# Gathered experts' down products as three fp32r passes, adaLN two pieces per step in the full experts, two more split gate blocks, and moved steps

## What is computed

```python
# first block, after the residual: 4 groups of 8 experts, top-1 group, top-2 experts in it
for n in range(N_EXPERTS):                       # 32 experts, 1024 -> 2 x 256 -> 1024
    a, b = jnp.split(h @ w_up[n], 2, axis=-1)
    out = out + combine[:, n:n + 1] * ((jax.nn.silu(a) * b) @ w_down[n])
# second block, per layer
mod = (silu(c) @ w_ada[l] + b_ada[l]).reshape(B, N_MOD, D_MODEL)       # adaLN
hn = rms_norm(h, g_ffn1[l]) * (1.0 + sc1) + sh1
h = h + 0.5 * (1.0 + gt1) * swiglu(hn, w_ffn1_in[l], w_ffn1_out[l])
```

## Time and profile before

| what | value |
|---|---|
| median of 3 runs | 1892.06 us |
| the profiled execution | 1889.99 us |
| its span, first to last instruction | 1888.2 us |
| TensorE busy | 1841.8 us (98%) |
| VectorE busy | 1173.6 us (62%) |
| ScalarE busy | 780.9 us (41%) |
| mean granted TensorE clock | 0.994 of full |
| read from and written to memory | 206 GB/s over the span |

### The profile page before, as it was taken

The page is one execution under the profiler, slowest core; times in us unless marked ns, Lnnn a source line. Parts: engine busy times, 40 slices in busy tenths (PEclk is TensorE's granted clock), DMA queues, the critical chain, the costliest instruction groups (busy, mean ns, idle before and its releaser), DMA issues.

```text
span 1888.2 us, 29939 instructions
## 1 busy us (share of the span) xinstructions
PE 1841.8 (98%) x12476; PEld 1661.0 (88%) x12476; DVE 1173.6 (62%) x1777; ACT 780.9 (41%) x1081; POOL 0.2 (0%) x4
## 2 busy tenths in 40 slices
PE   9999999899999999999999999999999999989999
PEld 8879889788866668999988889999999997879999
DVE  3875456566666656877547458776876547545543
ACT  2325442534444445434443234344443444324432
POOL 0000000000000000000000000000000000000000
PEclk9999999899999999999999999999999999999999
DMA  8334311566899986876530057876686341043451
GB/s 316 132 130 158 137 68 35 239 233 241 321 395 370 376 320 236 342 302 260 199 134 23 23 204 287 331 301 258 256 320 253 157 157 45 6 152 133 181 201 68
DMA packets 65222, 391.59 MB, mean 207 GB/s; under 512 B 7360, under 2 KB 7488, under 8 KB 27328
## 3 DMA queue, kind: packets, MB, share of 16 engines
q1 hardware_dynamic: 64800, 389.61, 53.4%
q10 hardware_dynamic: 288, 0.08, 0.0%
HBM read 388.61 MB, written 1.05 MB: 206 GB/s over the span
## 4 chain that ended last, share of the span: by engine, by line
PE 88%; DVE 7%; ACT 2%; issue 1%; DMA 1%; DVEq 0%; SPq 0%; ACTq 0%
PE bank L510 87%; DVE region L2219 1%; PE bank L551 1%; ACT w_hi L1452 1%; DMA slab<-in_w_ffn_in 1%; DVE slab_low L1900 0%; DVE region L2182 0%; DMA slab<-in_w_up 0%; DVE region L1913 0%; DVE tiny L2181 0%; DVE region L2505 0%; DVE region L2482 0%; DVE region L2503 0%; DVE region L2173 0%; DVE region L2501 0%
## 5 line engine op out<-in xcount | busy, mean ns | idle before, releaser
L1900 DVE TENSOR_TENSOR slab_low<-slab,w_hi 128x2048 fp32r<-128x2048 f32 x152 | 348.2, 2292 | 201.8 <-ACT w_hi L1452 201.5
L510 PE MATMUL bank<-h_hi,w_hi 128*128 128x256 f32 x1408 | 391.6, 281 | 0.0
L510 PE MATMUL bank<-h_hi,slab_low 128*128 128x256 f32 x1408 | 390.9, 281 | 0.0
L510 PE MATMUL bank<-h_lo,w_hi 128*128 128x256 f32 x1408 | 380.2, 281 | 0.0
L1452 ACT ACTIVATE w_hi<-slab 128x2048 fp32r<-128x2048 f32 x152 | 291.0, 1916 | 151.1 <-DMA slab<-in_w_ffn_in 72.9
L510 PEld LDWEIGHTS bank<-h_hi,slab_low 128*128 128x128 f32 x1408 | 269.5, 191 | 0.0
L510 PEld LDWEIGHTS bank<-h_hi,w_hi 128*128 128x128 f32 x1408 | 264.7, 188 | 0.4
L510 PEld LDWEIGHTS bank<-h_lo,w_hi 128*128 128x128 f32 x1408 | 257.6, 188 | 0.0
L510 PE MATMUL bank<-gT_hi,d_hi 128*128 128x256 f32 x832 | 234.0, 281 | 0.8 <-DVE gT_lo L2097 0.8
L510 PE MATMUL bank<-gT_lo,d_hi 128*128 128x256 f32 x832 | 233.7, 281 | 0.0
L510 PE MATMUL bank<-gT_hi,d_low 128*128 128x256 f32 x832 | 233.6, 281 | 0.0
(11 more groups left out here) (279 smaller groups left out, 2826.0 us busy)
## 6 DMA issues: line engine op xcount, KB each, us to landing
slab<-in_w_ffn_in SPq DMA_DIRECT2D x88, 1024.0 KB, 8.6
slab<-in_w_up SPq DMA_DIRECT2D x64, 1024.0 KB, 8.8
region<-in_w_ada SPq DMA_DIRECT2D x112, 512.0 KB, 6.6
region<-in_w_ffn_out SPq DMA_DIRECT2D x44, 1024.0 KB, 4.8
region<-in_w_down SPq DMA_DIRECT2D x32, 1024.0 KB, 5.5
slab<-in_w_in SPq DMA_DIRECT2D x23, 1024.0 KB, 4.8
slab<-in_w_mix_in SPq DMA_DIRECT2D x20, 1024.0 KB, 7.9
hT<-in_w_ada SPq DMA_DIRECT2D x32, 512.0 KB, 5.7
```

What stands on the lines that cost most here:

```text
L510: return nc.tensor.matmul(o, lhsT, rhs, start=start, stop=True, skip_group_check=True)
L1900: V_.tensor_tensor(slab_low[slot][:, :], slab[slot][:, :], w_hi[h % 3][:, :].bitcast(F), ALU.subtract)\
```

## The change

- `down_few` becomes three fp32r passes: ScalarE converts each gathered expert's down weights (`down_high` at the end of its own step), VectorE subtracts them (`down_low`, right behind `hidden`) and makes `gT_lo` for these experts too; `d_hi` alternates between two buffers, `gT_few` goes, and `permT` moves to `rsB` and the router's weights. `bank_free` waits for `gt_lo` for every expert.
- `ada_slot` gives two pieces per step in the experts' stage: 32 pieces in steps 1 to 16. `ADA_PLAN`'s rate, the two places and the order of SyncE's loads stay.
- `GATES_PLAIN` goes from 4 to 2: 22 gate blocks of 24 are split, in 11 slabs.
- In stage 1 the rotations of q and k (`qka_normed`) come after all 16 blocks, and the doubled keys after the four key blocks; VectorE makes `in_lo` and the first gate slab's low part ahead of the norms of the memory's q and k.
- At the start of the experts: `keep_warm(5)` becomes 3; ScalarE brings in `htok_lo` and `permT` ahead of `up_high(0)`; c is loaded after the second unit's up weights.

```diff
@@ -162,7 +162,7 @@
...
 GATHER_PLACES = 3
-GATES_PLAIN = 4
+GATES_PLAIN = 2
 VALUES = P + 8
...
@@ -181,10 +181,6 @@
...
     halves: list
-
-    @property
-    def split(self):
-        return self.kind != "few"
...
@@ -223,7 +219,7 @@
...
     _, _, n, rate = ADA_PLAN[seg]
-    return [p for p in range(n) if 1 + p // rate == r]
+    return [p for p in range(n) if 1 + p // (rate if seg else 2) == r]
...
@@ -367,7 +363,7 @@
...
         second = zone(27 * KB + NT * N_EXP, NT * PER_GROUP).rearrange("p (t e) -> p t e", t=NT)
-        permT = zone(28 * KB, (N_GROUP - 1) * T).rearrange("p (i t) -> p i t", i=N_GROUP - 1)
+        permT = [rsB[:, 0:T], rsB[:, T:2 * T], part["router"][:, 0:T]]
         hg_hi, hg_lo = split_zone("hg_hi", 72 * KB, [KD, GS]), split_zone("hg_lo", 84 * KB, [KD, GS])
...
@@ -378,8 +374,6 @@
...
         gT_lo = [parts_at(f"gT_lo{b}", [2, T], silu_at + 4096 * b + 2048) for b in range(2)]
-        gT_few = [nc.alloc_sbuf_tensor_at(f"gT_few{b}", [P, 2, P], F, offset=silu_at + 4096 * b)
-                  for b in range(2)]
         act_s, gu_s = lnt[:, 0:T], lnt[:, T:2 * T]
...
@@ -463,11 +457,7 @@
...
-            return sum(len([x for x in u.steps if x <= s]) for u in UNITS if u.split)
-
-        def split_units(u):
-
-            return sum(1 for x in UNITS[:u + 1] if x.split)
+            return s + 1
...
@@ -486,7 +476,7 @@
...
-            return 0 if unit.seg == 0 else unit.u % 2
+            return 0 if unit.kind == "full" else (unit.u + 1) % 2
...
@@ -759,10 +749,8 @@
...
                     pe.wait_ge(S["gut"], old + 1)
-                elif unit.split:
+                else:
                     pe.wait_ge(S["gt_lo"], low_steps(old))
-                else:
-                    pe.wait_ge(S["gt_hi"], old + 1)
...
@@ -794,7 +782,7 @@
...
                 b = unit.u % 2
-                pe.wait_ge(S["dlo_ready"], split_units(unit.u))
+                pe.wait_ge(S["dlo_ready"], unit.u + 1)
                 pe.wait_ge(S["gt_lo"], low_steps(unit.steps[-1]))
...
@@ -813,15 +801,18 @@
...
                 b = unit.u % 2
-                pe.wait_ge(S[f"d_in{b}"], 16 * (unit.u // 2 + 1))
-                pe.wait_ge(S["gt_hi"], unit.steps[-1] + 1)
+                pe.wait_ge(S["dlo_ready"], unit.u + 1)
+                pe.wait_ge(S["gt_lo"], low_steps(unit.steps[-1]))
                 if unit.x == 0 and unit.group > 1:
                     pe.wait_ge(S["y_copied"], 2 * (unit.group - 1))
-                rows_ = d_raw[b].rearrange("p (j d) -> p j d", j=2)
+                hi = d_hi[d_hi_of(unit)][:, :].rearrange("p (j d) -> p j d", j=2)
+                lo = d_low[b][:, :].rearrange("p (j d) -> p j d", j=2)
                 for j in range(2):
                     for half in range(2):
-                        m = mm(bank[2 + half][:, :], gT_few[b][:, j, :], rows_[:, j, half * 512:(half + 1) * 512],
-                               unit.x == 0 and j == 0)
+                        o, cols = bank[2 + half][:, :], slice(half * 512, (half + 1) * 512)
+                        mm(o, gT_hi[b][:, j, 0:P], hi[:, j, cols], unit.x == 0 and j == 0)
+                        mm(o, gT_hi[b][:, j, 0:P], lo[:, j, cols])
+                        m = mm(o, gT_lo[b][:, j, 0:P], hi[:, j, cols])
                     if j == 0 and middle:
...
@@ -833,13 +824,13 @@
...
                     m = mm(bank[4 + d // 2][:, (d % 2) * T:(d % 2 + 1) * T], y_few[:, d * P:(d + 1) * P],
-                           permT[:, i - 1, :])
+                           permT[i - 1])
                     if i == N_GROUP - 1:
...
             def down(unit, middle=None):
-                if unit.split:
+                if unit.kind != "few":
                     down_split(unit, unit.steps[0] == SLOTS_OF[unit.seg][0][2], middle,
...
@@ -848,7 +839,7 @@
...
                 slabs_of(members[0])
-                keep_warm(5)
+                keep_warm(3)
                 for s in range(2):
...
@@ -983,21 +974,17 @@
...
                     pair_sum(sq[:, 5, :])
-                if b == 15:
-                    pe.wait_ge(S["qka_normed"], w("qka_normed"))
-                    for x in range(2):
-                        pair_sum(B1["qa"][:, 2 * x:2 * x + 2, :], "rot", "dve")
-                    pair_sum(B1["ka"], "rot", "dve")
                 conv(b) if b < 8 else queries(b - 8) if b < 12 else memory(b - 12)
+            pe.wait_ge(S["qka_normed"], w("qka_normed"))
+            for x in range(2):
+                pair_sum(B1["qa"][:, 2 * x:2 * x + 2, :], "rot", "dve")
+            pair_sum(B1["ka"], "rot", "dve")
             for i in range(KD):
                 pe.wait_ge(S["memh"], w("memh"))
-            keys = projection(B1["memh"], 4, "act")
-            for b in range(4):
-                if b == 2:
-                    pe.wait_ge(S["ka_roped"], w("ka_roped"))
-                    for x in range(2):
-                        pair_sum(B1["ka"], f"dup{x}")
-                keys(b)
+            project(B1["memh"], 4, "act")
+            pe.wait_ge(S["ka_roped"], w("ka_roped"))
+            for x in range(2):
+                pair_sum(B1["ka"], f"dup{x}")
             vslab = [arrive().rearrange("p (k c) -> p k c", k=KD) for _ in range(2)]
...
@@ -1455,7 +1442,7 @@
...
                 act.wait_ge(S[f"d_in{b}"], 16 * (unit.u // 2 + 1))
-                k = unit.u - (1 if unit.seg == 0 else 2)
+                k = unit.u - (1 if unit.kind == "full" else 2)
                 if k >= 0:
...
@@ -1499,7 +1486,7 @@
...
                     src = place(s)[:, 0:T].rearrange("p (a b) -> p a b", a=2)
-                    dst = gT_hi[b][:, :, t * P:(t + 1) * P] if unit.split else gT_few[b][:, :, :]
+                    dst = gT_hi[b][:, :, t * P:(t + 1) * P]
                     nc.scalar.activation(dst, src, ACT.Copy).then_inc(S["gt_hi"], 1)
...
@@ -1520,7 +1507,7 @@
...
                         up_high(unit.halves[0] + 2)
-                        if unit is not members[0] and UNITS[unit.u - 1].split:
+                        if unit is not members[0] and UNITS[unit.u - 1].kind == "full":
                             down_high(UNITS[unit.u - 1])
...
@@ -1528,6 +1515,8 @@
...
                         up_high(unit.halves[1] + 2)
+                    if unit is not None and unit.kind == "few":
+                        down_high(unit)
                     if s == 0:
...
@@ -1629,10 +1618,9 @@
...
             for c in range(4):
-                if c == 2:
-                    for x in range(2):
-                        evac(B1["kdup"][:, x, :])
                 evac(B1["km"][:, c, :])
+            for x in range(2):
+                evac(B1["kdup"][:, x, :])
             act.wait_ge(S["read_by_act"], w.n["read_by_act"])
...
@@ -1701,20 +1689,20 @@
...
                     evac(htok_hi[:, t, x * 512:(x + 1) * 512], 512)
+            for t in range(NT):
+                for x in range(2):
+                    evac(htok_lo[:, t, x * 512:(x + 1) * 512], 512)
+            act.wait_ge(S["read_by_act"], w.n["read_by_act"])
+            act.sem_inc(S["tok_ready"], 1)
             act.wait_ge(S["router_top2"], w("router_top2"))
...
             m.then_inc(S["router_exp"], 1)
+            evac(rsB[:, :], 512)
+            evac(permT[2])
             up_high(0)
-            for t in range(NT):
-                for x in range(2):
-                    evac(htok_lo[:, t, x * 512:(x + 1) * 512], 512)
-            act.wait_ge(S["read_by_act"], w.n["read_by_act"])
-            act.sem_inc(S["tok_ready"], 1)
             up_high(1)
-            evac(permT[:, 0:2, :].rearrange("p i t -> p (i t)"), 512)
-            evac(permT[:, 2, :])
             moe()
...
@@ -1903,7 +1891,7 @@
...
                 b = unit.u % 2
-                dve.wait_ge(S["dhi_ready"], split_units(unit.u))
+                dve.wait_ge(S["dhi_ready"], unit.u + 1)
                 V_.tensor_tensor(d_low[b][:, :], d_raw[b], d_hi[d_hi_of(unit)][:, :].bitcast(F), ALU.subtract)\
...
@@ -2037,8 +2025,6 @@
...
                     unit = unit_of(s)
-                    if not unit.split:
-                        return
                     b, t = unit.u % 2, s - unit.steps[0]
...
@@ -2062,12 +2048,16 @@
...
                         hidden(x)
+                    few = bool(pending) and unit_of(pending[0]).kind == "few"
+                    if few:
+                        down_low(unit_of(pending[0]))
+                        turned_low(pending[0])
                     if unit is not None and t == 0:
                         up_low(unit.halves[0] + 2)
-                        if unit is not members[0] and UNITS[unit.u - 1].split:
+                        if unit is not members[0] and UNITS[unit.u - 1].kind == "full":
                             down_low(UNITS[unit.u - 1])
-                    for x in pending:
-                        turned_low(x)
+                    if pending and not few:
+                        turned_low(pending[0])
                     if unit is not None and unit.x == 1 and unit.group > 1:
...
```

(15 more changed lines are left out.)

## The result

The changed kernel takes 1952.78 us (median of 4 runs, 1952.35 to 1953.58) against 1892.72 us for the kernel before beside it: ratio 1.0317, interval 1.0299 to 1.0335. It is slower by 60 us. The sign was forecast, the size was not: 1928 was the number and 1941 the end of the range.

The account below looks back on a forecast made before the run. TensorE, with 88% of the chain of waits, was taken as the bound. Stage 1 -4.7, start +2.3, turns +49.0, clock +1.6 and gathered experts -12.1 gave +36.1 on 1889.99: 1926.1, as median 1928, range 1912 to 1941 us.

Parts of the forecast that it names:

- Stage 1, -4.7: Stage 1: the last memory block covers the wait for q and k rotations, two more split blocks gain: -4.7 us.
- Start, -6.2: Start of the experts: with waits and loads removed from ahead, TensorE starts at 335.1 instead of 341.31: -6.2 us.
- Net +2.3: Expert 1's second step: later pieces delay its load, so the start's gain is lost again, net +2.3 us.
- The turns, +49.0: Full experts: up weights queue behind two pieces, so TensorE's resume-to-resume turn takes 24.3 us, not 17.3; seven turns, +49.0.
- slab issued at 371.26, ScalarE let go at 376.51: 5.25: Full experts: the landing inside each turn, from SyncE's load issue to ScalarE's release, priced at 5.25 us.
- 6.9 us, or the clock stays down: Rival, full experts: slabs land in 6.9 us or clock stays low both half steps, +1.65 per turn: 1940, chance 0.14.
- Gathered experts, -12.1+1.6: Gathered experts: fp32r down products, less losses at group changes and end, -12.1 us; low clock after the last turn, +1.6.
- The two changes of group: Gathered experts: VectorE's copy of a finished group's output comes 1.2 us late at two group changes, +2.5 us.
- The end: End of the gathered experts: the last down product waits for its own low parts, about +1.5 us.
- ScalarE and VectorE as a bound: Rival, gathered experts: ScalarE and VectorE become the bound, gain gone, +12 to 16 us: 1942, chance 0.06.
- As meant: Rival, full experts: weights arrive in time despite the queue, so they cost nothing: -21.8 us, 1870, chance 0.07.
- The clock stays up: Rival, full experts: the stall comes but the clock stays up, turns of 22.7 us: +23.3 us, 1915, chance 0.16.

Follow-up runs that it names:

- the loads first: The changed kernel with SyncE issuing the up weights of expert n+1 ahead of the adaLN pieces of expert n: 1871.66 us, ratio 0.989.
- the clock held up: The changed kernel with 16 unread products ahead of the wait for `bank_free` in each full expert's second step: 1936.38 us.

## Why the prediction was wrong, step by step

**Stage 1, -4.7: right.** `h_hi` starts at 307.93 instead of 312.74, -4.8.

**Start, -6.2: right.** TensorE starts the experts at 330.13, not 341.31: -11.2 with stage 1, against -10.9.

**Step 1, "Net +2.3": 1.5 short.** Expert 1's second step starts at 368.82, -0.9 against -4.7+2.3 = -2.4. Its load took 7.14 from issue to let go, not 5.2.

**The turns, +49.0: the mechanism right, one term mis-sized.** The failing step is "slab issued at 371.26, ScalarE let go at 376.51: 5.25", taken as "the case with an adaLN piece just ahead, as here". But here the two pieces of a step are used 1.15 us apart, and so two are issued just ahead of the load. The row showed the landing with one. With one piece ahead a load lands in 5.9 on average (5.25 is below the least of the eight, 5.44), with two in 7.4. The term is 2.15 too small. The rest of the turn was 0.6 too small, most of it clock: the first half step was priced from a row at 0.56 and runs at 0.51 (window above), with ScalarE's turned copy 5.06 us after the resumption in this turn and later in the next ones (from one `gT_lo` to the next 6.05 us at first, 6.62 at the end). 27.08-24.3 = 2.78, seven times: 19.5 of the 24.8 us of the miss. And the range could have been wider from rows in hand: beside the landing's median of 6.9, taken as the bound, shows a largest of 8.5, and landing and clock were let out one at a time, as one rival ("6.9 us, or the clock stays down"), though they add.

**Gathered experts, -12.1+1.6: 2.9 short.** From the down products of expert 7 to the last scattering, 490.84 to 721.30 before and 558.35 to 781.22 now: -7.6. A step is 8.61, not 8.56, so 0.61 per expert was gained, not 0.67: 1.4 in all. The two changes of group cost 1.0 each more than before and one step ahead of the second another 0.55, +2.6 against +2.5 forecast. The clock behind the last pause costs 2.5, not 1.6: the first 26 of expert 7's down products take from 558.35 to 563.98, 5.6 us, where before they took 3.1 (490.84 to 493.91). The end costs 2.0, not 1.5. ScalarE and VectorE as a bound did not come.

```profile
558.35:562.35 4.00, 4.00 (x19) 4.00 (x20) 4.00 (x4) 2.75 (x3) 0.00 (x0) 0.50 0.49 205
```

By the Trainium skill, TensorE: Matmul & The Clock Gate, section "Wait — 56ns, not 53.3ns?", the pitch is 215.7 ns and the stage would have gained 4.4 us more. The rows above still show 0.23 us (594.01 to 594.24), and the stage gained less than forecast, not more.

**The layers, 0: +2.5.** The instructions are the same. The granted clock is at half for 6.6 us where it was low for about 4 (windows of the changed kernel, then of the one before):

```profile
1161.00:1167.60 6.60, 5.34 (x13) 4.30 (x14) 3.53 (x7) 1.89 (x3) 0.00 (x0) 0.52 1.03 417
```
```profile
1102.00:1106.00 4.00, 3.46 (x9) 2.78 (x9) 2.81 (x6) 1.62 (x3) 0.00 (x0) 0.58 1.03 421
```

What sets the length of this stretch of low clock was not found. From the last scattering to the end the traces of the twelve kernels here take 1166.7 to 1169.9 us, though none of the edits touches the layers. A difference of up to 3 us between two of these kernels should be read from the stage it is in.

**Sum.** 19.5 + 1.5 + 2.9 + 2.5 = 26.4, less 1.6, since the profiled run is 0.4 below its median and not 2.07: the 24.8 us from 1928 to 1952.8.

**Rivals.** "As meant" was priced at 1870 and rested on the load being in time: with the loads first it is, and the kernel takes 1871.7. "The clock stays up" was priced at 1.6 us a turn; with the clock held up it is 2.1. The rival of 1940 named the term that failed, the landing, and priced it at 11.6 of the 24.8 us; it had a chance of 0.14.

## What to carry to other kernels

In a queue that waits in place, look at what stands behind each wait: a filler load that waits for its buffer must not stand ahead of a load on the critical path. Give a transfer the price of all the bytes issued just ahead of it in its queue, count the issues of a pair one by one, and take bounds from the row's largest value, with terms that can go wrong together let out together. Where a stall can't be removed, products that nobody reads can still buy back the clock.

## What the runs showed of the hardware

- A 1 MB load (128 x 8 KB) on SyncE's queue is slowed by what is ahead of it: it lands in 4.7 us with nothing ahead, 5.9 with one piece of 0.52 MB (128 rows of 4 KB), 7.4 with two. It is not slowed by what is behind it: 7.4 us with two more megabytes behind it, 7.5 with none.
- The Trainium skill, DMA: Bandwidth & Descriptors, section "Anatomy of one DMA — SWDGE (gpsimd) path", gives 2.0 us + bytes/436e3 for another issue path, an estimate of 4.4 us for 1 MB. On SyncE's queue the traces show 4.7 for such a load with nothing ahead, 0.3 more.
- While the pieces were under way, 250 to 303 GB/s moved (388 to 392 us in the windows above) at a DMA share of 0.88 to 1.03; the gathered stage reached 419 at 1.01. The share alone does not give the rate.
- 16 small products in a pause of 8 us kept the granted clock at full (1.00 in the window behind it), where without them it was 0.51 for the first half step.
